# Stick-breaking mixer: four pairs' values projected by token ahead of the loop, ten projection pieces a pair inside it

## What is computed

```python
def _stick_breaking_attention(q, k, v):
    ...
    def block(args):
        qb, start = args
        z = jnp.einsum("bhqd,bhkd->bhqk", qb.astype(jnp.float32), k32) * scale
        q_pos = start + jnp.arange(Q_BLOCK)
        mask = key_pos[None, :] < q_pos[:, None]
        log_beta = jax.nn.log_sigmoid(z)
        log_1m = jnp.where(mask, jax.nn.log_sigmoid(-z), 0.0)
        suffix = lax.cumsum(log_1m, axis=3, reverse=True) - log_1m
        wts = jnp.where(mask, jnp.exp(log_beta + suffix), 0.0)
        return jnp.einsum("bhqk,bhkd->bhqd", wts, v32)
    ...

def _sb_mixer(h, w_qkv, w_out):
    bsz, s, _ = h.shape
    qkv = (h @ w_qkv.astype(h.dtype)).reshape(bsz, s, 3, SB_HEADS, SB_HEAD_DIM)
    qkv = qkv.transpose(2, 0, 3, 1, 4)
    o = _stick_breaking_attention(qkv[0], qkv[1], qkv[2])
    o = o.transpose(0, 2, 1, 3).reshape(bsz, s, D_MODEL)
    return o @ w_out.astype(h.dtype)
```

## Time and profile before

| | |
|---|---|
| median of 3 runs | 2158.82 us (2157.7 to 2159.76) |
| the profiled execution, its own time | 2155.77 us |
| its span | 2154.0 us |
| the mixer's part, from the first projection to the last `values` | 527.8 to 744.6 us of the span |

### The profile page before, as it was taken

The page is one execution under the profiler, slowest core; times in us unless marked ns, Lnnn a source line. Parts: engine busy times, 40 slices in busy tenths (PEclk is TensorE's granted clock), DMA queues, the critical chain, the costliest instruction groups (busy, mean ns, idle before and its releaser), DMA issues.

```text
span 2154.0 us, 25179 instructions
## 1 busy us (share of the span) xinstructions
PE 2109.1 (98%) x10295; PEld 1527.5 (71%) x10295; DVE 1018.2 (47%) x1510; ACT 747.6 (35%) x1070; POOL 144.8 (7%) x149
## 2 busy tenths in 40 slices
PE   9999999999999999999999999999999999999897
PEld 7878888888777778888888766777787544444333
DVE  7875433445666564434446655555564312112123
ACT  7773222223555442222234545433333001010012
POOL 0220000001000010000010010162101000000000
PEclk9999999999999999999999999999999999999999
DMA  5233233223221122233234121241245899999996
GB/s 215 78 101 105 86 90 116 94 77 115 68 70 57 62 98 95 76 122 98 74 113 147 42 69 54 63 97 59 75 149 221 359 399 414 419 420 419 419 419 258
DMA packets 86610, 350.81 MB, mean 163 GB/s; under 512 B 9312, under 2 KB 21856, under 8 KB 62176
## 3 DMA queue, kind: packets, MB, share of 16 engines
q1 hardware_dynamic: 82320, 342.48, 43.1%
q0 software_dynamic: 2192, 2.63, 0.9%
q10 hardware_dynamic: 1984, 4.10, 0.5%
HBM read 347.06 MB, written 2.10 MB: 162 GB/s over the span
## 4 chain that ended last, share of the span: by engine, by line
PE 86%; DVE 4%; DMA 4%; ACT 3%; issue 2%; ACTq 0%; POOL 0%; DVEq 0%; SPq 0%; POOLq 0%
PE PS L2090 20%; PE PS L2092 19%; PE PS L2091 19%; PE PS L2470 9%; PE PS L2507 4%; DMA SL<-in_wgu_dram 4%; PE PS L2133 2%; PE PS L2454 1%; PE PS L2207 1%; DVE WL L1588 1%; PE PS L2302 1%; PE PS L2320 1%; PE PS L2221 1%; PE PS L2231 1%; DVE XC L1655 1%
## 5 line engine op out<-in xcount | busy, mean ns | idle before, releaser
L2090 PE MATMUL PS<-HH,WH 128*128 128x512 f32 x1392 | 553.7, 398 | 4.4 <-ACT GT L1299 1.4
L2092 PE MATMUL PS<-HH,WL 128*128 128x512 f32 x1392 | 542.6, 390 | 0.0
L2091 PE MATMUL PS<-HL,WH 128*128 128x512 f32 x1392 | 542.1, 389 | 0.0
L1588 DVE TENSOR_TENSOR WL<-RAW,WH 128x1024 fp32r<-128x1024 f32 (+4 forms) x302 | 344.6, 1142 | 304.6 <-ACT WH L1288 303.8
L1288 ACT ACTIVATE WH<-RAW 128x1024 fp32r<-128x1024 f32 (+4 forms) x302 | 286.3, 950 | 321.3 <-PE PS L2092 297.6
L2090 PEld LDWEIGHTS PS<-HH,WH 128*128 128x128 f32 x1392 | 261.3, 188 | 74.8 <-issue 17.5
L2092 PEld LDWEIGHTS PS<-HH,WL 128*128 128x128 f32 x1392 | 261.2, 188 | 55.9
L2091 PEld LDWEIGHTS PS<-HL,WH 128*128 128x128 f32 x1392 | 261.5, 188 | 53.5 <-issue 1.4
L2470 PE MATMUL PS<-SL,XS 128*64 128x512 f32 x960 | 231.4, 597 | 8.7 <-DMA SL<-in_wgu_dram 8.7
L2470 PEld LDWEIGHTS PS<-SL,XS 128*64 128x64 f32 x960 | 71.1, 136 | 127.9 <-issue 123.5
L2090 PE MATMUL PS<-MH,WH 128*128 128x512 f32 x352 | 136.9, 389 | 0.0
(11 more groups left out here) (343 smaller groups left out, 2667.9 us busy)
## 6 DMA issues: line engine op xcount, KB each, us to landing
SL<-in_wgu_dram SPq DMA_DIRECT2D x120, 1024.0 KB, 22.7
SL<-in_wdn_dram SPq DMA_DIRECT2D x54, 1024.0 KB, 24.7
RAW<-in_w_dram SPq DMA_DIRECT2D x46, 512.0 KB, 3.5
RAW<-in_wg_dram SPq DMA_DIRECT2D x44, 512.0 KB, 3.5
RAW<-in_wu_dram SPq DMA_DIRECT2D x44, 512.0 KB, 3.4
RAW<-in_wd_dram SPq DMA_DIRECT2D x32, 384.0 KB, 3.1
RAW<-in_wqkv_dram SPq DMA_DIRECT2D x24, 512.0 KB, 3.5
RAW<-in_wd_dram SPq DMA_DIRECT2D x32, 320.0 KB, 2.9
```

The costliest lines, as they stand in the source:

```text
L1588: e.tensor_tensor(wl, raw, wh.bitcast(F), ALU.subtract).then_inc(*wlo.did("u", u))
L2090: e.matmul(out, wh[:, w], xh, start=k == 0, stop=False)
L2091: e.matmul(out, wh[:, w], xl, start=False, stop=False)
L2092: m = e.matmul(out, wl[:, w], xh, start=False, stop=k == g.total - 1)
```

## The change

The values of the first four pairs (c below NNAT = 4) are no longer groups of `project()`. Ahead of everything in the mixer a new step sequence, `by_token`, computes them for all four pairs at once: four units of w_qkv, each with two of the eight 128-row blocks and 512 columns, are the moving side, and 128 tokens of HH or HL are the stationary side. The four token blocks fill four banks (96 matmuls of 512 columns in all), three matmuls in a bank and then the next bank. The row norms are needed with tokens on the partitions: `rest_t` is four matmuls of SA with a column of ones, a root on ACT and a reciprocal on DVE over 4 columns. `vt_out` scales the four banks into VA, two on ACT and two on DVE. A unit of this kind is loaded in runs of 1 KB instead of 4 KB. `values` of these pairs reads VA. `rest(o, 2)` stands behind `rest_t`.

`project()` has two groups for each of the pairs 0 to 3, three for 4 to 7. Nine pieces instead of thirteen are done ahead of the loop, and place D has three pieces instead of five, except for the last pair. In all there are 96 pieces instead of 112. The pairs 4 to 7 are still turned by `natural`.

```diff
...
 NBACK = 4
 NGATE = 4
 NWARM = 21
+NNAT = 4
 
 VEC = {}
 _at = 0
...
 def sb_order(o):
     def project():
         for c in range(DC):
-            for i in range(3):
+            for i in range(2 if c < NNAT else 3):
                 def done(c=c, i=i):
-                    if c == 0 and i == 0:
-                        rest(o, 2)
                     o.add("qkv", c, i)
                     o.release(("qkv", c, i), "scaled", "qkv", c, i)
 
-                work = o.lin_steps(("qkv", c, i), [("wqkv", (8 * i + c,), 8)], "h", done, fresh=c + i == 0, size=2)
+                work = o.lin_steps(("qkv", c, i), [("wqkv", (8 * i + c,), 8)], "h", done, size=2)
                 step(work)
-                if c and i == 0:
+                if c > NNAT and i == 0:
                     natural(c - 1)
                 yield
                 yield from work
...
             work = o.lin_steps(("out", 1, c), [("wbo", (c, slice(None), slice(0, DC - 1)), DC - 1)], "o", done,
                                fresh=c == 0, size=2)
             step(work)
-            if c == 0:
+            if c == 0 and NNAT < DC:
                 natural(DC - 1)
             yield
             yield from work
+
+    def by_token(g):
+        for tb in range(4):
+            o.claim("vt", g, tb)
+        for j in range(4):
+            u = o.unit("wqkv", (slice(16 + 4 * g, 20 + 4 * g), slice(None), slice(2 * j, 2 * j + 2)), 8)
+            o.add("split", u + AHEAD)
+            o.add("vt", g, j, u)
+        if g == 0:
+            o.claim("rst")
+            o.add("rest_t")
+            o.release(("rst",), "root", "rest_t")
+            rest(o, 2)
+        for tb in range(4):
+            o.add("vt_out", g, tb)
+            o.release(("vt", g, tb), ("lo", "hi")[tb % 2], "vt", g, tb)
 
     def natural(c):
         o.claim("vn", c)
...
         o.release(("val", c), "lo", "o", c)
 
     o.add("sb_consts")
+    for g in range(NNAT // 4):
+        by_token(g)
     at = [o.freed.get(b) for b in range(6)]
     o.only(6, 7)
     fill = project()
-    step(fill, 13)
+    step(fill, 9)
     for c in range(DC):
         o.add("scores", c, at if c == 0 else [])
         o.add("stick", c, 0)
...
         o.add("turn_w", c, 0)
         step(fill, 2)
         o.add("turn_w", c, 1)
-        step(fill, 5)
+        step(fill, 5 if c == DC - 1 else 3)
     values(DC - 1)
     finish(fill)
     for b in range(6):
...
                 if u >= NRAW:
                     e.wait_ge(*wlo("u", u - NRAW))
                 src = I[name][idx]
+                by_k = name == "wqkv" and len(idx) == 3
                 if name in ("wbo", "w2o") and len(idx) == 3 and isinstance(idx[2], int):
                     src = src.rearrange("c p n -> p c n")
-                elif name == "wout" and isinstance(idx[0], slice):
+                elif by_k or name == "wout" and isinstance(idx[0], slice):
                     src = src.rearrange("c p a n -> p c a n")
                 dst = RAW[u % NRAW][:, 0:nt * 128]
-                dst = (dst.rearrange("p (c a b) -> p c a b", c=4, a=2) if name == "wout" and isinstance(idx[0], slice)
+                dst = (dst.rearrange("p (c a b) -> p c a b", c=4, a=2) if by_k or name == "wout" and isinstance(idx[0], slice)
                        else dst.rearrange("p (a b) -> p a b", a=nt))
                 e.dma_start(dst, src).then_inc(*d_raw[u % NRAW].did(u))
             for i, src in enumerate(loads):
...
                     e.activation(S1[l][:, z, :], G1[l][:, z, :], ACT.Silu).then_inc(*silu.did("f", l, i))
                     e.wait_ge(*mul("f", l, i))
                     e.activation(MH[l][:, f, :], U1[l][:, z, :], ACT.Copy).then_inc(*hi.did("m", l, half, f))
+                elif kind == "rest_t":
+                    e.wait_ge(*red("rest_t"))
+                    e.activation(RT, bank("rst")[:, 0:4], ACT.Sqrt, bias=vec("eps", 0), scale=1.0 / D).then_inc(
+                        *root.did("rest_t"))
+                elif kind == "vt_out" and a[1] % 2:
+                    g, tb = a
+                    e.wait_ge(*lin("vt", g, tb))
+                    e.wait_ge(*rsv("rest_t"))
+                    e.activation(VA[:, g, tb, :], bank("vt", g, tb), ACT.Copy, scale=RT[:, tb:tb + 1]).then_inc(
+                        *hi.did("vt", g, tb))
                 elif kind == "scores":
                     c, _ = a
                     e.wait_ge(*att("sc", c))
...
                 elif kind == "sb_consts":
                     e.tensor_copy(IB[:, 0:128], ident).then_inc(*stick.did("ident"))
                     e.tensor_copy(IB[:, 128:256], cst("nmask")).then_inc(*stick.did("consts"))
+                elif kind == "rest_t":
+                    e.wait_ge(*root("rest_t"))
+                    e.reciprocal(RT, RT).then_inc(*rsv.did("rest_t"))
+                    e.wait_ge(*rsv("rest_t"))
+                elif kind == "vt_out" and a[1] % 2 == 0:
+                    g, tb = a
+                    e.wait_ge(*lin("vt", g, tb))
+                    e.tensor_scalar(VA[:, g, tb, :], bank("vt", g, tb), RT[:, tb:tb + 1], None, ALU.mult).then_inc(
+                        *lo.did("vt", g, tb))
                 elif kind == "qkv":
                     c, i = a
                     dve_scaled(e, QK[c % 2][:, i, :], bank("qkv", c, i), o.last(("qkv", c, i)), ("qkv", c, i),
...
                     e.wait_ge(*freed("vn", c))
                     e.wait_ge(*scaled("qkv", c, 2))
                     pe_turn(e, ("vn", c), [QK[z][:, 2, 128 * j:128 * j + 128] for j in range(4)])
+                elif kind == "vt":
+                    g, j, u = a
+                    e.wait_ge(*wlo("u", u))
+                    for k in (2 * j, 2 * j + 1):
+                        wh, wl = (W[u % NSPL][:, :].rearrange("p (c a b) -> p a c b", c=4, a=2)[:, k % 2] for W in (WH, WL))
+                        if g == 0:
+                            e.wait_ge(*lo("h", 2, k))
+                        for tb in range(4):
+                            if k == 0 and o.before["vt", g, tb]:
+                                e.wait_ge(*freed("vt", g, tb))
+                            xh, xl = (H[:, k, 128 * tb:128 * tb + 128] for H in (HH, HL))
+                            e.matmul(bank("vt", g, tb), xh, wh, start=k == 0, stop=False)
+                            e.matmul(bank("vt", g, tb), xh, wl, start=False, stop=False)
+                            m = e.matmul(bank("vt", g, tb), xl, wh, start=False, stop=k == DC - 1)
+                            if k == DC - 1:
+                                m.then_inc(*lin.did("vt", g, tb))
+                    if j < 3:
+                        m.then_inc(*lin.did("u", u))
+                    else:
+                        lin.also("u", u)
+                elif kind == "rest_t":
+                    if o.before["rst",]:
+                        e.wait_ge(*freed("rst"))
+                    e.wait_ge(*sa(2, 7))
+                    for tb in range(4):
+                        m = e.matmul(bank("rst")[:, tb:tb + 1], SA[:, 128 * tb:128 * tb + 128], ones[:, 0:1], start=True,
+                                     stop=True, skip_group_check=True)
+                    m.then_inc(*red.did("rest_t"))
                 elif kind == "scores":
                     c, before = a
                     z = c % 2
...
                     c, = a
                     e.wait_ge(*freed("val", c))
                     e.wait_ge(*soft("t", c, 1))
-                    e.wait_ge(*turned("vn", c))
+                    if c >= NNAT:
+                        e.wait_ge(*turned("vn", c))
+                    elif c == 0:
+                        e.wait_ge(*lo("vt", 0, 2))
+                        e.wait_ge(*hi("vt", 0, 3))
                     for j in range(4):
                         for p in range(2):
-                            r = 128 * j + 64 * p
-                            m = e.matmul(bank("val", c)[64 * p:64 * p + 64, 128 * j:512], VN[c % 2][:, r:r + 64],
+                            r = 64 * p
+                            V64 = VA[:, 0, j, 128 * c + r:128 * c + r + 64] if c < NNAT else VN[c % 2][:, 128 * j + r:128 * j + r + 64]
+                            m = e.matmul(bank("val", c)[64 * p:64 * p + 64, 128 * j:512], V64,
                                          WT[p][:, OFF[j]:OFF[j] + WID[j]], start=j == 0, stop=j == 3, skip_group_check=True)
                     m.then_inc(*att.did("val", c))
                 elif kind == "natural":
...
```

More of the change, by code:

```diff
@@ L998, in program @@
         VN = [sb(f"VN{i}", [128, T], F, ph) for i in range(2)]
+        VA = sb("VA", [128, NNAT // 4, 4, 512], F, ph)
         ZP = [sb(f"ZP{i}", [128, 1280], F, ph) for i in range(2)]
@@ L1107, in cst @@
             return C[:, CST[n] + a:CST[n] + a + w]
+        RT = SM[:, 0:4]
         ident, ones, bones, anti = cst("ident"), cst("ones"), cst("bones"), cst("anti")
```

## The result

The changed kernel took 2165.46 us (median of 7 runs, 2163.25 to 2166.94); the kernel before, run beside it on the same chip, 2158.69 us (7 runs, 2155.94 to 2159.76). The ratio is 1.0036, 95% interval 1.0027 to 1.0046: 7.8 us slower by the ratio, between 5.8 and 9.9; the two medians lie 6.8 apart. The profiled execution of the changed kernel took 2166.94 us, with a span of 2165.0 us, against 2155.77 and 2154.0 before.

What follows compares the result with a forecast made beforehand. The prediction took PE, busy 98% of the span at full clock, as the bound; its terms summed to +9.95 us, taking the median of 2158.8 to 2168.7 us, with a range of 2161.5 to 2173.5.

Steps and rivals of the forecast that it cites:

- pace of the new matmuls: Opening of the mixer: 32 triples at the output mix's 0.70 us against 0.68, +0.7 us.
- four turns of values gone: PE in the loop: four turns of the values removed at 0.53 us each, -2.1 us.
- head of the mixer: Start of the mixer: `rest_t` and the norms' matmul take 1.65 us against 1.9 before, -0.2 us.
- turns 1 and 5: Loop: PE waits for OL's bank and ahead of the second `turn_w`, 2 x 2.45 = +4.9 us.
- turn 3: Loop: `natural` of pair 4 in place C also waits for its scaling on DVE, +3.15 us.
- turn 4: Loop: `natural` of pair 5, behind the second `turn_w`, waits for a scaling queued behind a WL, +0.3 us.
- turn 7: Last loop turn: a split and the copy for `natural` precede the running sums; PE waits 3.0 against 0.8, +2.2 us.
- behind the loop: After the loop: `values` of pair 7 stands one short piece ahead of a group awaiting OL, +0.7 us.
- odd turns: Loop: a new group's split in place A precedes head 1's running sums on DVE, moving everything behind by 2.45 us.
- R3: Rival: new matmuls run slower, from four-run moving side or falling clock, +12 or +22 us, 2180 to 2190 us; chance 4%.
- R1: Rival: the split doesn't hold up the chain, so all loop waits vanish; -1.1, 2157.7 us; chance 8%.
- R2: Rival: only one of the two waits appears, half of the loop's 10.5; +4.7, 2163.5 us; chance 10%.

## Why the prediction held

2168.7 us was forecast with +9.95 in the mixer; the mixer has +9.52, and the median is 3.2 us lower. By terms, the predicted ones with the 0.1 for the change back to split matmuls put where it stands:

| term | predicted | measured |
|---|---|---|
| pace of the new matmuls | +0.7 | 0 |
| four turns of values gone | -2.1 | -1.76 |
| head of the mixer | -0.2 | -0.20 |
| turns 1 and 5 | +4.9 | +4.86 |
| turn 3 | +3.25 | +3.15 |
| turn 4 | +0.4 | +0.42 |
| turn 7 | +2.3 | +2.15 |
| behind the loop | +0.7 | +0.89 |

The step that carried it is that of the odd turns. It put the WL of place A on DVE's clock ahead of the running sums and got 2.45 us. The trace shows that very row, and the sums 2.43 us late. The kernel before with two more pieces ahead shows it once more, 2.48 a turn, without anything else of the change. Even turns kept their time, as the counting of pieces said: 21.44 us against the predicted 21.3. Turns alternate as named, and the releasers are those named: QK in turn 3, the Exp in 1, 5 and 7, and OL in place A four times, in turn 7 without its name. The idle ahead of the Exp is 0.94, 0.94 and 0.97 us where the prediction asked for above 1; with the overlap of 0.16 it comes to that. In turn 7 the waiting that the prediction gave as 3.0 us in one stands in three places, 1.08, 0.41 and 0.97.

Four terms or sentences were off.

*The new matmuls, +0.7.* The price was taken from the nearest row, the mix with a triple every 0.70 us. Here it is 0.68. That four runs of 128 columns on the moving side, or a change of bank every three matmuls, cost anything is disproved for this kernel: 0.2267 us each over 96 of them at clock 1.00. The mechanism of rival R3 didn't occur in these matmuls, nor did the clock go up and down there as the Trainium skill, "TensorE: Matmul & The Clock Gate", section "A second HAM failure mode: psum-queue depth-cycling", reports for its kernel. That section puts it down to short idles of PE between the groups, which the prediction left out; here the window shows PE busy for all of the 21.76 us.

*A turn of values, 0.53.* It was the distance from its start to that of the scores. By the lengths of turns that differ in nothing else, it is 0.44: so the start-to-start distance holds something that the scores would have paid anyway. -2.1 should have been -1.8. It takes back half of what the first term gave, so by luck the sum came out closer than these two terms.

*The clock.* R3 argued that PE had been idle 2.2 us at a stretch "with no slice below full clock". A slice of the page is 54 us long and can't show three slow microseconds. A window of 3 us at the end of that wait does, in the same trace:

```profile
1323.00:1326.00 3.00, 2.85 (x23) 2.52 (x24) 1.75 (x4) 1.22 (x4) 0.00 (x0) 0.61 0.54 156
```

The kernel before thus had such a fall already. For the prediction it made no difference, since the changed kernel's own waits in the loop, 1.70 and 1.73 us at most, left the clock at 1.00 in both of its profiles; and the fall shown above cost next to nothing where it stood, as the last section tells. But the reason that was given was none, and the kernel with the splits put off shows that one more step of this size could have cost 1.6 us more.

*The opening as a price.* R3 took 0.35 us for the slowest matmuls of 512 columns, the mean of the 21 in the opening. In the timeline these have two paces: starts at 2.76, 3.19 and 3.61, so 0.43 apart, and later at 6.62 and 6.84, 0.22 apart. So the lower figure of R3, +12, stands for no pace of its own. 0.43 is also the spacing at half speed behind the wait of 2.32 us, though the view gives 1.00 for the opening; why it does isn't shown.

R1, that the split doesn't hold the chain up, fell with the rows of turn 1. R2, that half appears, fell with the table above: no wait was missing. By the ratio the whole time grew by less than the mixer's 9.5 in the first comparison (7.8) and about by it in the second (9.3); what the 1.7 between are isn't shown, and both intervals hold 9.5.

What makes the change slower is not the projection by token. It gives 0.44 us for each pair, and with the loop kept in step and one split moved, all eight pairs by token are faster than the kernel before. What costs in this change is that ten pieces a turn aren't a multiple of four: groups start at other places of the list in every second turn. Being in step is not enough by itself, as the kernel with eight and then twelve pieces shows, whose mixer still takes 5.5 us more than before.

## What to carry to other kernels

Where a loop's side work comes in groups of k pieces, changing the number of pieces in a turn to one that isn't a multiple of k changes where in each engine's queue a group's start stands; count the phase for every turn and put each instruction that a group's start issues on the clock of the chain that it is queued ahead of. Moving that instruction helps only past all the work that waits at its new place: put behind one chain it delayed the next. A step that cost half a microsecond beside other work can cost three times as much where its result has to pass a busy queue.

## What the runs showed of the hardware

The moving side of a split matmul in four runs of 128 columns, 1 KB apart in SBUF, goes at the same 0.2267 us as one run of 512, also with a change of bank every three.

The same idle stretch sometimes lowers TensorE's clock and sometimes not. PE waits 2.18 us for GT at about 1320 to 1350 us in each of the ten profiled executions of this study. In the 3 us from the end of that wait the granted clock was 0.59 in the kernel before, 0.74, 0.61 and 0.69 in three others, and 1.00 in the remaining six. The window of the changed kernel's first profile, to be held against the one of the kernel before in the section on why the prediction held:

```profile
1333.68:1336.68 3.00, 2.12 (x24) 1.72 (x24) 1.59 (x4) 1.26 (x3) 0.00 (x0) 1.00 0.46 168
```

A window of 3 us is not the whole story either. In three of the six the clock fell all the same, 5 to 6 us behind the end of that wait, and PE had waited another 1.34 us, for PG, between the two. The changed kernel's second profile, in which the wait for GT ends at 1332.56:

```profile
1338.00:1341.00 3.00, 3.00 (x7) 1.77 (x8) 1.08 (x4) 2.98 (x8) 0.00 (x0) 0.50 0.00 0
```

Only in three executions did it stay at 1.00 for 15 us: the changed kernel's first, the one with eight and then twelve pieces, and all eight pairs by token with no split moved. What a fall costs depends on the work that it meets. From the end of the wait for GT to the start of the next group of split matmuls are 12.46 to 12.50 us in these three. It is 12.54 in the kernel before and 12.63 in another, where the fall came within 1 us, 13.99 to 14.02 in the three in which it came late, and 16.24 and 16.10 in the last two, in which half speed lasted 10 us: up to 3.7 us more.

The lower value within a window is 0.50, the 1.2 GHz level, as behind the wait of 2.32 us above; at the end of one of 3.85 us it was 0.50 again; behind two of 1.70 and 1.73 us it stayed at 1.00. So a wait of some 2.2 us has a price of its length, and in some executions a second one, which ranged from nothing to 3.7 us. Which of them it will be, no run here tells in advance.
